# Ten modulation units in each projection half and none in the first routing of a two-layer hybrid backbone

## The reference, cut to what matters

```python
mod = einsum('bd,de->be', silu(cond), w_mod[i]) + b_mod[i]
sh1, sc1, g1, sh2, sc2, g2 = split(mod, 6, axis=-1)
h = modulate(rmsnorm(x, norm1_g[i]), sh1, sc1)
out = hgrn_mixer(h, ...) if i % 2 == 0 else fourier_mixer(h, ...)
x = x + g1[:, None, :] * out
h = modulate(rmsnorm(x, norm2_g[i]), sh2, sc2)
x = x + g2[:, None, :] * hier_moe(h, ...)
```

## Time and profile before

| | us |
|---|---|
| median of three runs | 1121.35 (1120.0 to 1122.34) |
| the profiled execution, its own time | 1121.53 |
| its span in the trace | 1119.7 |
| PE busy | 957.9 (86%) |
| DVE busy | 244.9 (22%) |
| ACT busy | 222.6 (20%) |
| POOL busy | 147.3 (13%) |

### The profile page before, as it was taken

The page is one execution under the profiler, slowest core; times in us unless marked ns, Lnnn a source line. Parts: engine busy times, 40 slices in busy tenths (PEclk is TensorE's granted clock), DMA queues, the critical chain, the costliest instruction groups (busy, mean ns, idle before and its releaser), DMA issues.

```text
span 1119.7 us, 21357 instructions
## 1 busy us (share of the span) xinstructions
PE 957.9 (86%) x8838; PEld 558.1 (50%) x8839; DVE 244.9 (22%) x544; ACT 222.6 (20%) x473; POOL 147.3 (13%) x243
## 2 busy tenths in 40 slices
PE   3799999999999996998799999199949999878760
PEld 2466455766455545554355555184435555434430
DVE  1100444101453244110011111521330110000005
ACT  1111012221002131122222222320311222221112
POOL 0000000100000110221111221300102212110112
PEclk9899999999999997999999999599959999998995
DMA  9965344276352646999999996830471999999953
GB/s 387 391 250 225 153 154 151 81 275 264 146 190 76 245 150 277 424 424 424 427 426 426 426 425 281 328 132 1 150 290 48 427 379 426 426 426 429 424 227 163
DMA packets 34185, 318.35 MB, mean 284 GB/s; under 512 B 6788, under 2 KB 9284, under 8 KB 16080
## 3 DMA queue, kind: packets, MB, share of 16 engines
q1 hardware_dynamic: 23024, 297.58, 65.0%
q0 software_dynamic: 7840, 15.18, 3.6%
q10 hardware_dynamic: 3264, 4.72, 1.2%
HBM read 309.11 MB, written 17.33 MB: 292 GB/s over the span
## 4 chain that ended last, share of the span: by engine, by line
PE 66%; DMA 23%; DVE 3%; ACT 3%; issue 3%; POOLq 1%; SPq 0%; POOL 0%; ACTq 0%; DVEq 0%
PE ps L857 16%; DMA ring<-in_moe_w_up 14%; PE ps L534 11%; PE ps L537 8%; PE ps L683 7%; PE ps L874 7%; DMA work<-hrow,gi 5%; PE ps L468 3%; DMA ring<-in_w_mod 2%; PE ps L625 2%; PE ps L821 1%; PE ps L769 1%; PE ps L510 1%; ACT ring L934 1%; PE ps L752 1%
## 5 line engine op out<-in xcount | busy, mean ns | idle before, releaser
L857 PE MATMUL ps<-ring,work 128*64 128x256 f32 x2432 | 293.3, 396 | 36.2 <-DMA ring<-in_moe_w_up 33.6
L857 PEld LDWEIGHTS ps<-ring,work 128*64 128x64 f32 x2432 | 186.1, 142 | 142.7 <-issue 49.4
L874 PE MATMUL ps<-ring,work 128*64 128x512 f32 x608 | 145.3, 598 | 0.0
L534 PE MATMUL ps<-ring 128*128 128x384 f32 x384 | 131.0, 493 | 5.2 <-ACT ring L934 5.2
L1410 DVE TENSOR_TENSOR work<-work,ps 128x128 f32<-128x128 f32 x76 | 21.9, 288 | 375.6 <-ACT work L1066 360.8
L537 PE MATMUL ps<-ring 128*128 128x512 f32 x192 | 99.0, 629 | 1.9 <-issue 1.9
L534 PEld LDWEIGHTS ps<-ring 128*128 128x128 f32 x384 | 71.4, 192 | 53.0 <-ACT ring L934 5.5
L683 PE MATMUL ps<-ring 128*128 128x512 f32 x192 | 84.4, 594 | 2.6 <-ACT ring L995 2.0
L468 PE MATMUL ps<-ring,scond 128*2 128x128 f32 x1536 | 51.1, 290 | 21.0 <-DMA ring<-in_w_mod 20.9
L874 PEld LDWEIGHTS ps<-ring,work 128*64 128x64 f32 x608 | 40.3, 136 | 55.2 <-issue 44.4
L1066 ACT ACT_TABLE_LOAD x38 | 48.8, 1283 | 48.4 <-issue 48.3
(11 more groups left out here) (157 smaller groups left out, 721.9 us busy)
## 6 DMA issues: line engine op xcount, KB each, us to landing
ring<-in_moe_w_gate SPq DMA_DIRECT2D x32, 2048.0 KB, 20.4
ring<-in_moe_w_up SPq DMA_DIRECT2D x32, 2048.0 KB
ring<-in_moe_w_down SPq DMA_DIRECT2D x32, 2048.0 KB, 33.2
ring<-in_w_mod SPq DMA_DIRECT2D x24, 2048.0 KB, 21.1
ring<-in_hgrn_w_in SPq DMA_DIRECT2D x10, 2048.0 KB
ring<-yrows SPq DMA_DIRECT2D x6, 1024.0 KB, 7.0
ring<-in_hgrn_w_out SPq DMA_DIRECT2D x2, 2048.0 KB
ring<-in_fourier_w_out SPq DMA_DIRECT2D x2, 2048.0 KB
```

What stands on the lines that cost most here:

```text
L534: last = mm(bank[:, 0:T], W[:, k, c * P:(c + 1) * P], hT[:, k, :], start=(k == 0), stop=(k == KD - 1))
L857: last = mm(ps[h * SLOTS:(h + 1) * SLOTS, GU_BANK[j], 0:2 * P], xt[:, k % 4, k // 4 * SLOTS:(k // 4 + 1) * SLOTS], Wgu[:, :, at:at + P], s ...
L874: last = mm(ps[h * SLOTS:(h + 1) * SLOTS, Y_BANK, :], hidT[:, j, q * SLOTS:(q + 1) * SLOTS], slot_d(S[2])[:, 2 * q + j, h * C512:(h + 1) * ...
```

## The change

All units from 4 on run inside the projections, ten in each half: a product after steps 7, 21, 35 and so on (counted from 0), its turn six steps later. Routing has none. All units from 7 on pass through slot 2, and the loads stand in `STREAM` in the order in which the slots come free. Expert 1 is asked for as the two output weights leave slots 0 and 1. DVE's row copies and column additions are spread over ten units instead of eight (`heads`, not shown: it has the same operations in another order), and POOL writes the rows of units 22 and 23 in the second half.

```diff
         def mod_slot(U):
-            return [3, 4, 5, 2, 3, 2, 3][U] if U < 7 else 2 if U < 20 else [2, 0, 1, 2][U - 20]
+            return [3, 4, 5, 2, 3, 2, 3][U] if U < 7 else 2
...
-        STREAM = ([("mod", U) for U in range(4)] + [("hgrn", 0), ("hgrn", 1), ("mod", 4), ("mod", 5), ("mod", 6),
-                  ("mod", 7), ("hgrn", 2), ("mod", 8), ("hgrn", 3), ("mod", 9), ("mod", 10), ("hgrn", 4), ("mod", 11),
-                  ("hgrn", 5), ("mod", 12), ("hgrn", 6), ("mod", 13), ("mod", 14), ("hgrn", 7), ("mod", 15),
-                  ("mod", 16), ("hgrn", 8), ("mod", 17), ("mod", 18), ("hgrn", 9), ("mod", 19), ("hgrn", 10),
-                  ("mod", 20), ("hgrn", 11)])
+        STREAM = ([("mod", U) for U in range(4)] + [("hgrn", 0), ("hgrn", 1), ("mod", 4), ("mod", 5),
+                  ("mod", 6), ("mod", 7), ("hgrn", 2), ("mod", 8), ("mod", 9), ("hgrn", 3), ("mod", 10), ("mod", 11),
+                  ("hgrn", 4), ("mod", 12), ("mod", 13), ("hgrn", 5), ("mod", 14), ("hgrn", 6), ("mod", 15), ("mod", 16),
+                  ("hgrn", 7), ("mod", 17), ("mod", 18), ("mod", 19), ("hgrn", 8), ("mod", 20), ("mod", 21),
+                  ("hgrn", 9), ("mod", 22), ("mod", 23), ("hgrn", 10), ("hgrn", 11)])
...
-        for u in (21, 22, 23):
-            place("mod", u, mod_slot(u))
...
-            for u in (21, 22):
-                sp.wait_ge(out_mm[0], [4, 6][u - 21])
-                mod_load(u)
-            sp.wait_ge(mod_mm, 21)
-            mod_load(23)
-            sp.wait_ge(mod_mm, 22)
-            expert_unit(0, 1, 2)
-            sp.wait_ge(mod_mm, 23)
-            expert_unit(0, 1, 0)
             sp.wait_ge(mod_mm, 24)
             expert_unit(0, 1, 1)
+            sp.wait_ge(out_mm[0], 4)
+            expert_unit(0, 1, 2)
+            sp.wait_ge(out_mm[0], 6)
+            expert_unit(0, 1, 0)
             moe_units(0)
...
+                            U, at = divmod(KD * m + k, 14)
+                            U += 4 + 10 * half
+                            if at == 7 and U < 14 + 10 * half:
+                                mod_next(U)
+                            if at == 13 and U < 14 + 10 * half and U in COLUMN_UNITS:
+                                mod_turn(U, 7)
                         n += 1
-                        if m % 2 == 1 and m < 16:
-                            mod_next(4 + 8 * half + m // 2)
-                        if m % 2 == 0 and m >= 2 and 4 + 8 * half + m // 2 - 1 in COLUMN_UNITS:
-                            mod_turn(4 + 8 * half + m // 2 - 1, 7)
...
-                pe.wait_ge(mod_evac, 20)
-                pe.wait_ge(col_set, turned_of(19) - 2)
+                pe.wait_ge(mod_evac, 24)
+                pe.wait_ge(col_set, turned_of(21) - 2)
...
-                if l == 0:
-                    pe.wait_ge(col_set, turned_of(19) - 2)
-                    for U in (20, 21):
-                        mod_product(U, 6 + U % 2)
...
-                if l == 0:
-                    for U in (20, 21):
-                        mod_turn(U, 6 + U % 2)
-                    for U in (22, 23):
-                        mod_product(U, 4 + U % 2)
...
-                if l == 0:
-                    for U in (20, 21):
-                        mod_evac_row(U, 6 + U % 2)
...
-            for U in (22, 23):
-                mod_columns(U - 2, 6 + U % 2)
-            for U in (22, 23):
-                mod_evac_row(U, 4 + U % 2)
...
-                    for U in (16, 17):
+                    for U in (16, 17, 22, 23):
                         gate_rows(U)
...
-            for U in (22, 23):
-                gate_rows(U)
```

## The result

The changed kernel is slower: 1133.12 us, median of 8 runs (1129.45 to 1135.36), against 1122.33 for 8 runs of the kernel before beside it, a ratio of 1.0085 with a 95% interval of 1.0062 to 1.0108, some 9.5 us (the two medians are 10.8 apart). The forecast was 1124.7, with 1130.5 as the upper end of the range: the sign was right, the size was not.

The account below looks back on a forecast made before the run. PE was taken to bound the projections, and weight loads the first expert stage up to expert 8. Terms +7.6 + 3.0 + 0.5 - 1.8 - 6.0 = +3.3 us gave 1124.7 beside the median, range 1119.5 to 1130.5.

Parts of the forecast that it names:

- Products, +7.6: Projections: four products moved in from the first routing at 1.86 us each, plus two more turns, add 7.6 us of PE.
- First wait, +3.0: First projection half: PE waits 2.2 us for unit 4's weights, plus 0.8 for a possibly slower clock behind it.
- Slot 2, +0.5: Projections, units from 7 on: loads get 9.2 us between products instead of 10.5, costing 0.5 us of waits.
- The dense thirds: Last third of each projection half, with small score matmuls: the sum held no extra stall there beyond the products.
- the rival: Last third of each projection half: PE's idle gaps double (+4.2 us) and the clock drops at unit 4's wait; 1129.8, chance 0.20.
- Routing, -1.8: First layer, first router matmul to first pass: without products 36.0 us as in layer 1, instead of 37.8.
- Expert stream, -6.0: First expert stage: ninth pass 104.4 us after the first instead of 110.4, limited by when expert 3 can be requested.

Follow-up runs that it names:

- four_twice: The kernel before with four of its products in the projections multiplied twice, loads and first routing unchanged: 1127.19 us, ratio 1.0033 to the kernel before.
- waits_out: The changed kernel with unit 4's product after 12 steps instead of 7 and unit 17's weights loaded ahead of a projection unit: 1127.50 us, 1.0035 to before.
- after_again: The changed kernel as it is, profiled and timed once more: 1133.63 us, ratio 1.0084 to the kernel before.
- expert1_held: The changed kernel with expert 1's three loads held back to where the kernel before issues them: 1132.88 us, ratio 1.0076 to the kernel before.

## Why the prediction was wrong in size

*Products, +7.6: right as a price.* One takes 1.84 to 1.86 us at full clock. Between kernels whose loads are out of the way the projections differ by 6.8 to 8.5 us; in four_twice they grew by only 4.6, with smaller gaps and a better clock beside the four products.

*First wait, +3.0: right in size, in part by luck.* The wait is 1.79 us (I said 2.2, bounds 1.7 to 2.6). I added 0.8 for a clock that might fall behind it, because 2.2 "lies between" the waits that cost clock and the one that didn't. It doesn't, it is below all of them (2.24, 2.27, 2.58), and the granted clock behind the wait was 1.00 in every window from 45 to 57 us. What came instead lies before the wait: the half clock at the start of the projections lasted longer, so that eight steps took 8.11 us, 2.8 more than at full clock, where the sixteen of before took 12.05, 1.5 more (10.59 at full clock). The same two us of before and of the changed kernel, with the granted clock third from the end:

```profile
43.00:45.00 2.00, 2.00 (x8) 1.21 (x7) 0.00 (x0) 0.00 (x0) 0.00 (x0) 1.00 0.99 414
43.00:45.00 2.00, 2.00 (x5) 1.13 (x4) 0.00 (x0) 0.00 (x0) 0.00 (x0) 0.60 0.97 407
```

*Slot 2, +0.5: the first step that failed.* I took the lower end "because the stretch of before that sends two together shows no wait". The order of loads was new, though, and at unit 17 a projection unit goes ahead of the modulation unit: 1.81 us of wait, 1.9 by waits_out. I had named 4 us as the upper bound.

*The dense thirds, counted at nothing beyond their products: the step that cost most.* I left it to the rival, with a chance of 0.20 and 1129.8 us. The rival is what happened, in a milder form: the gaps grew by 1.1 us in the first half and by 0.1 in the second, and the clock behind them did the rest; the first half's third grew by 4.4 us (6.3 in after_again) for one product and a turn (2.0). I had named the loads in flight as their companion and then didn't follow the new load order through that stretch. The runs show it: holding two loads and moving one product by five steps took 8.3 us off the projections (323.4 to 315.1). The Trainium skill (Runtime: NRT & Kernel Launch, on instruction fetch mechanics) says that code comes in 16 KB blocks, fetched ahead, and that the cost is mostly hidden. The profile's page agrees on the blocks: it counts 49 instruction packets with 0.80 MB. In these thirds it isn't hidden: the 51 gaps that end behind such a packet are 0.3 to 2.8 us long.

*Routing, -1.8: the third step that failed.* It came out at +0.2 here, and at 37.9 to 38.8 us in the five other profiles of the changed order that left expert 2's loads where they were. I took the second layer as the measure of the first, and the 1.8 between them as the price of the products. But the last thing that routing waits for is the gather. In before it took 8.3 us too, beside expert 1's loads, and PE idled 3.31 us for it with all products done (POOL and PE of before, the gather and the turn of its rows):

```profile
438.95 1.10 POOL L1534 DMA_INDIRECT work<-hrow,gi  x1 [0.88 <-POOL gi L1531]
447.25 1.11 PE L821 MATMUL ps<-first,work 128*128 128x128 f32 x4 [3.31 <-DMA work<-hrow,gi]
```

Without the products slot-finding ends no sooner (24.3 us after the router against 24.0), so the gather starts no sooner, and only a shorter gather could have shortened routing. It takes 8.3 us beside the loads, 3.5 without, and 5.9 in the second layer of before (832.28 to 838.16), where the loads have 2 us more of a start: they go out 15.5 us after the router there, and in the changed first layer 17.5 (443.89 - 426.38), since the last write of the token rows that they wait for landed 4.6 us after its issue, there 2.6. Why the writes differ stays open. The Trainium skill (DMA: Bandwidth & Descriptors, on arbitration) says that a DMA engine takes turns between its queues, packet by packet. The trace of expert1_held agrees, with 76 packets of the loads beside 75 of POOL's queue: the small transfer is served, but slowly.

*Expert stream, -6.0: right,* with 6.4, for the reason given: idle DMA until expert 3 is released, waits left before passes 7 to 9, and the ninth pass 103.98 us after the first (104.4). expert1_held shows the gain to be capped by that release.

Of the sum, +3.3, the projections missed 4.1 us and routing 2.0; -0.4 in the stream, -0.3 at the start and -0.9 in the second layer went the other way. That gives the profile's 7.9 but for rounding. The medians are 2.9 us further apart than the two profiled executions, because the changed kernel's lies 3.7 us below the median of its runs and that of before 0.8 below. What its longer executions spend the difference on stays open.

## To carry to other kernels

Moving work from one stage into another moves its loads too: write down, for each load of the new order, what is under way beside it, above all in stretches of many small matmuls and around a small transfer on which the path waits. Before a stage is said to get shorter by the work that leaves it, look at what it waits for last. Shifting loads, and two products with them, took 20 us off the changed kernel (1133.1 to 1113.3); the move itself was worth nothing that could be told. A stage that has its like elsewhere in the kernel is a measure only if what runs beside it is the same.

## What was not expected of the hardware

A small gather (one indirect DMA) takes 3.3 to 3.5 us alone and, in the first layers where weight loads run beside it, 7.8 to 10.0. In expert1_held its queue shared the engines with them packet by packet, 75 against 76 in 3 us, and it was done 12.8 us before the last of them.

PE's gaps at the diagonal scores, 2.1 to 2.8 us in the changed order, fell to 0.9 or less when the weight loads beside them were moved by a few us. All 51 such gaps in the dense thirds end 1.2 to 1.5 us after a 16 KB instruction packet. Where no gap was over 1.2 us the granted clock of the third was 1.00 in nine of nine; with a longer one it was 0.96 to 0.98 in twelve of 17.
